# Three RMS norms taken in two columns, eight low-half subtractions given to VectorE, the gathered rows at a multiple of 512 bytes, two constant matrices left out

## The reference

```python
def first_block(x, mem, ...):
    x = x + conv_mixers(rms_norm(x, norm_mix_g[l]), w_in[l], ...)          # gated convolutions, w_mix_out
    x = x + memory_cross_attention(rms_norm(x, norm_xa_g[l]), mem_n, w_q[l], w_kv[l], w_xo[l])
    x = x + peer_ffn(rms_norm(x, norm_peer_g[l]), w_peer_q[l], peer_subkeys[l], peer_u[l], peer_v[l])
    return rms_norm(x, final_norm_g)

def peer_ffn(h, w_pq, subkeys, u, v):
    ...   # 8 heads; each token picks 16 of 16384 experts per head by two top-16 lists of 128 sub-keys
    act = gelu(einsum('chkd,cd->chk', u[experts], h)) * gates
    return einsum('chk,chkd->cd', act, v[experts])

def second_block(x, positions, ...):
    h = rmsnorm(x, pre_norm_mix)
    ...   # windowed attention and latent attention, two gates
    x = x + rmsnorm(merged @ w_out, post_norm_mix)
    y = square(relu(rmsnorm(x, pre_norm_mlp) @ w_up)) @ w_down
    return x + rmsnorm(y, post_norm_mlp)

def rms_norm(x, g):
    return x * rsqrt(mean(x * x, axis=-1) + 1e-6) * g
```

## Time and profile before

| | |
|---|---|
| three runs | 1491.06, 1491.51, 1495.69 us (median 1491.51) |
| the profiled execution | 1493.7 us, span 1491.9 us |
| mean granted TensorE clock | 0.961 |
| busy: PE, DVE, ACT, POOL | 88%, 66%, 35%, 38% of the span |
| gathered bytes | 268.45 MB |

### The profile page before, as it was taken

How to read it: one execution, slowest core, us unless ns; L and a number is a source line. 1 busy time by engine, 2 the same in 40 slices (tenths; PEclk the granted TensorE clock), 3 DMA queues, 4 the chain that set the end, 5 groups by cost and what they waited for, 6 DMA issues and landing times.

```text
span 1491.9 us, 25940 instructions
## 1 busy us (share of the span) xinstructions
PE 1312.2 (88%) x10024; PEld 1253.7 (84%) x10024; DVE 979.4 (66%) x2091; ACT 519.7 (35%) x990; POOL 561.5 (38%) x348
## 2 busy tenths in 40 slices
PE   6999999999888797796968886878899999889996
PEld 5999999988888797796968786878785889889996
DVE  4679986766688585859585768755424447683574
ACT  4633456445442121211112221211226455434341
POOL 1588843221455455354535364545002000022220
PEclk9999999999999989898999899999999999999999
DMA  6555544452389999999999999999830135245450
GB/s 238 213 192 175 188 168 168 158 196 87 112 327 420 421 422 422 422 422 422 422 420 420 421 420 422 422 422 422 359 142 0 57 114 174 100 156 201 162 195 32
DMA packets 58088, 397.39 MB, mean 266 GB/s; under 512 B 6289, under 2 KB 9873, under 8 KB 10385
## 3 DMA queue, kind: packets, MB, share of 16 engines
q0 software_dynamic: 36864, 268.45, 43.3%
q1 hardware_dynamic: 21136, 127.76, 24.2%
HBM read 395.14 MB, written 1.05 MB: 266 GB/s over the span
## 4 chain that ended last, share of the span: by engine, by line
PE 52%; DMA 21%; DVE 13%; issue 8%; ACT 3%; POOL 2%; DVEq 0%; POOLq 0%; ACTq 0%; SPq 0%
DMA rows_late<-peer_uv_dram,stage 21%; PE bank L703 11%; PE bank L705 11%; PE bank L704 11%; PE bank L677 6%; PE bank L914 6%; DVE rows_late L1870 4%; ACT w_hi L1110 2%; PE bank L689 1%; POOL rows_late L620 1%; PE bank L808 1%; DVE hid L2054 1%; POOL w_lo L516 1%; DVE rstd L1442 1%; PE bank L832 1%
## 5 line engine op out<-in xcount | busy, mean ns | idle before, releaser
L516 POOL TENSOR_TENSOR w_lo<-raw,w_hi 128x2048 fp32r<-128x2048 f32 x49 | 228.7, 4669 | 489.8 <-ACT w_hi L1110 489.8
L914 PE MATMUL bank<-h_norm,rows_late 128*128 128x128 f32 x2816 | 328.8, 279 | 30.3 <-ACT h_norm L1274 30.3
L914 PEld LDWEIGHTS bank<-h_norm,rows_late 128*128 128x128 f32 x2816 | 324.9, 196 | 33.4 <-ACT h_norm L1274 33.4
L1870 DVE SCALAR_TENSOR_TENSOR rows_late<-rows_late,squares 128x1024 f32<-128x1024 f32 x176 | 213.8, 1229 | 134.2 <-DMA rows_late<-peer_uv_dram,stage 125.1
L914 PE MATMUL bank<-h_norm,rows_early 128*128 128x128 f32 x1280 | 176.4, 305 | 94.7 <-ACT h_norm L1274 94.7
L914 PEld LDWEIGHTS bank<-h_norm,rows_early 128*128 128x128 f32 x1280 | 170.3, 219 | 101.2 <-ACT h_norm L1274 101.1
L620 POOL DMA_INDIRECT rows_late<-peer_uv_dram,stage x165 | 196.8, 1193 | 131.7 <-PE bank L914 77.7
L1110 ACT ACTIVATE w_hi<-raw 128x2048 fp32r<-128x2048 f32 x102 | 194.3, 1906 | 59.7 <-PE bank L705 49.7
L703 PE MATMUL bank<-x_hi_b,w_hi 128*128 128x256 f32 x640 | 186.9, 292 | 13.8 <-DVE x_lo_b L1474 4.9
L703 PE MATMUL bank<-x_hi_a,w_hi 128*128 128x256 f32 x672 | 191.6, 285 | 4.7 <-DVE x_lo_a L1472 2.3
L704 PE MATMUL bank<-x_lo_a,w_hi 128*128 128x256 f32 x672 | 190.8, 284 | 0.0
(11 more groups left out here) (303 smaller groups left out, 2016.9 us busy)
## 6 DMA issues: line engine op xcount, KB each, us to landing
raw<-w_in_dram SPq DMA_DIRECT2D x28, 1024.0 KB, 5.0
raw<-w_up_dram SPq DMA_DIRECT2D x16, 1024.0 KB, 4.9
raw<-w_down_dram SPq DMA_DIRECT2D x16, 1024.0 KB, 4.9
rows_late<-w_in_dram SPq DMA_DIRECT2D x10, 1024.0 KB, 13.6
raw<-w_kv_dram SPq DMA_DIRECT2D x8, 1024.0 KB, 4.9
raw<-w_peer_q_dram SPq DMA_DIRECT2D x8, 1024.0 KB, 5.0
raw<-sc_w_out_dram SPq DMA_DIRECT2D x4, 1024.0 KB, 4.9
raw<-cf_w_pw_dram SPq DMA_DIRECT2D x4, 1024.0 KB, 4.9
```

What stands on the lines that cost most here:

```text
L516: api.tensor_tensor(ring(w_lo, i), ring(raw, i), ring(w_hi, i).bitcast(F32), ALU.subtract).then_inc(w_lo_ready[LO_BY[i][0]], 1)
L914: mm = nc.tensor.matmul(ct(Y_ACC[c][t // 4], t % 4, P), expert_rows(k)[:, D + t * P:D + (t + 1) * P], ct(diag, k % DIAGS, P), start=False, ...
L1870: w_.scalar_tensor_tensor(out=row, in0=row, scalar=1.0, in1=h_tok[:, c * D:(c + 1) * D], op0=ALU.mult, op1=ALU.mult, accum_out=pre[:, side ...
```

## The change

It has four parts. (1) `BY_DVE` begins at load 32 ("k", 0) and no longer at load 62: eight subtractions that GpSimd made (loads 32, 35, 38, 44, 47, 50, 53 and 56: the first and last of k, the third of sc, the first and last of mix, the third of q, the second of xo, the first of pq) are VectorE's; loads 40, 41 and 58 to 61 stay with GpSimd by `DVE_BUSY`. (2) For the norms in `BY_TOKEN` the squares are the stationary operand and one column of mean_d the moving one: the mean stands in two columns, one per chunk of tokens. ACT and VectorE work on two elements per partition, and TensorE spreads the two columns over the rows again with two products by the identity, into PSUM, which VectorE reads in its place of rstd. (3) mean_q and mean_kv go; the small norms use mean_d and a scale in the root. (4) With them gone and row_pad in, rows_late begins at byte 61,440, a multiple of 512; rows_early and all else behind it move by the same 704 bytes.

```diff
-BY_DVE = range(LOAD_OF["pq", 12], LOAD_OF["up", 6])
+BY_DVE = range(LOAD_OF["k", 0], LOAD_OF["up", 6])
...
+BY_TOKEN = ("peer", "post_mix", "post_mlp")
...
-        mean_q = sb("mean_q", P)
-        mean_kv = sb("mean_kv", P)
...
+        root_col = sb("root_col", NC)
+        rstd_col = sb("rstd_col", NC)
...
+        sb("row_pad", 64)
         (rows_late,) = shared(("rows_late", ROWS_LATE * 2 * D, F32))
...
+        RSTD_HALVES = [psum[7][:, SEQ + c * P:SEQ + (c + 1) * P] for c in range(NC)]
...
             g.memset(mean_d[:], 1.0 / D).then_inc(filled, 1)
-            g.memset(mean_q[:], 1.0 / 256).then_inc(filled, 1)
-            g.memset(mean_kv[:], 1.0 / 128).then_inc(filled, 1)
...
-                    mm = nc.tensor.matmul(STAT[:, 0:SEQ], mean_d[:], ct(squares, k), start=(k == 0), stop=(k == tiles[-1]))
+                    if name in BY_TOKEN:
+                        for c in range(NC):
+                            mm = nc.tensor.matmul(STAT[:, c:c + 1], ct(squares, k)[:, c * P:(c + 1) * P], mean_d[:, 0:1],
+                                                  start=(k == c == 0), stop=(k == tiles[-1] and c == NC - 1))
+                    else:
+                        mm = nc.tensor.matmul(STAT[:, 0:SEQ], mean_d[:], ct(squares, k), start=(k == 0), stop=(k == tiles[-1]))
                 mm.then_inc(stat_ready, 1)
+
+            def spread(name):
+
+                pe.wait_ge(inverted, BY_TOKEN.index(name) + 1)
+                for c in range(NC):
+                    nc.tensor.matmul(RSTD_HALVES[c], rstd_col[:, c:c + 1].to_broadcast([P, P]), ident,
+                                     start=True, stop=True).then_inc(rstd_spread, 1)
...
             stat_sum("peer")
+            spread("peer")
...
-            lora_stat("kv_square", 1, mean_kv, 0)
+            lora_stat("kv_square", 1, 0)
...
-                s.activation(root_buf[:], STAT[:, 0:SEQ], ACT.Sqrt, bias=eps[:, 0:1]).then_inc(rooted, 1)
+                out, n = (root_col, NC) if name in BY_TOKEN else (root_buf, SEQ)
+                s.activation(out[:], STAT[:, 0:n], ACT.Sqrt, bias=eps[:, 0:1]).then_inc(rooted, 1)
...
-                s.activation(root_buf[:], acc(name, 0), ACT.Sqrt, bias=eps[:, 0:1]).then_inc(acc_freed["act"], 1)
+                s.activation(root_buf[:], acc(name, 0), ACT.Sqrt, bias=eps[:, 0:1], scale=float(DT // kt)).then_inc(acc_freed["act"], 1)
...
                 dve.wait_ge(rooted, ROOTS.index(name) + 1)
-                link(w_.reciprocal(rstd[:] if to is None else to, root_buf[:]))
+                if name in BY_TOKEN:
+                    w_.reciprocal(rstd_col[:], root_col[:]).then_inc(inverted, 1)
+                    dve.wait_ge(rstd_spread, NC * (BY_TOKEN.index(name) + 1))
+                    return RSTD_PS
+                to = rstd[:] if to is None else to
+                link(w_.reciprocal(to, root_buf[:]))
+                return to
```

More of the change, by code:

```diff
@@ L480, in two_blocks @@
         inverse_ready = sem("inverse_ready")
+        inverted = sem("inverted")
+        rstd_spread = sem("rstd_spread")
         counts = {}
@@ L834, in sum_values @@
                                  start=False, stop=True).then_inc(acc_ready, 1)
-            pe.wait_ge(filled, 6)
+            pe.wait_ge(filled, 4)
             stat_sum("mix")
@@ L948, in _, with lora_stat @@
             rot = k_of("rot")[NOPE:QHB, 0:QHB]
-            def lora_stat(name, kt, ones, first):
+            def lora_stat(name, kt, first):
                 out = open_tile(name, 0)
@@ L954, in lora_stat @@
                     pe.wait_ge(lora_squared, first + k + 1)
-                    mm = nc.tensor.matmul(out[:, 0:SEQ], ones[:], ct(lora_squares, first + k),
+                    mm = nc.tensor.matmul(out[:, 0:SEQ], mean_d[:], ct(lora_squares, first + k),
                                           start=(k == 0), stop=(k == kt - 1))
@@ L1025, in _ @@
                 mm.then_inc(acc_ready, 1)
-            lora_stat("q_square", 2, mean_q, 1)
+            lora_stat("q_square", 2, 1)
             linear_whole("qa", range(2), "w_in_2", 8, 256)
@@ L1051, in _ @@
             stat_sum("post_mix")
+            spread("post_mix")
             for half in range(2):
@@ L1062, in _ @@
             stat_sum("post_mlp")
+            spread("post_mlp")
             assert tile[0] == len(TILES)
@@ L1185, in _ @@
             square("mix", lambda k: act.wait_ge(x_landed[k // 4], 16), x_res)
-            act.wait_ge(filled, 8)
+            act.wait_ge(filled, 6)
             root("mix")
@@ L1323, in square_lora, with root_of_lora @@
                 s.activation(ct(lora_squares, first + n), ct(latent, n), ACT.Square).then_inc(lora_squared, 1)
-            def root_of_lora(name):
+            def root_of_lora(name, kt):
                 wait_tile(act, name, 0)
-                s.activation(root_buf[:], acc(name, 0), ACT.Sqrt, bias=eps[:, 0:1]).then_inc(acc_freed["act"], 1)
+                s.activation(root_buf[:], acc(name, 0), ACT.Sqrt, bias=eps[:, 0:1], scale=float(DT // kt)).then_inc(acc_freed["act"], 1)
             drain("ckv", 0, c_kv[:])
@@ L1336, in _ @@
                 square_lora("cq", i, 1, c_q)
-            root_of_lora("kv_square")
+            root_of_lora("kv_square", 1)
             wait_tile(act, "ka", 0)
@@ L1347, in _ @@
             act.wait_ge(lora_normed, 1)
-            root_of_lora("q_square")
+            root_of_lora("q_square", 2)
             for i in range(2):
@@ L1482, in norm_split @@
             def norm_split(name, src, gain, dst, x):
-                rstd_of(name)
+                by = rstd_of(name)
                 k = NORMS[NORM_AT[name]][1]
@@ L1488, in norm_split @@
                         done(w_.scalar_tensor_tensor(out=ct(dst, i), in0=ct(src, i), scalar=v(gain, i),
-                                                     in1=rstd[:], op0=ALU.mult, op1=ALU.mult), normed)
+                                                     in1=by, op0=ALU.mult, op1=ALU.mult), normed)
                     if i:
@@ L1515, in _ @@
             split_all("h1", h_norm)
-            dve.wait_ge(filled, 6)
+            dve.wait_ge(filled, 4)
             for i in range(8):
```

## The result

The changed kernel takes 1477.13 us (median of four runs, 1476.33 to 1480.8), the kernel before 1493.18 beside it. The ratio is 0.9897, 95% interval 0.9872 to 0.9922: by the ratio 15.4 us, against a forecast of 8.1. The profiled execution has a span of 1475.1 us.

A forecast was written before the change was run, and what follows sets the result against it. The prediction took the gather stage to be bound by its transfers at 421 GB/s, so gains had to come from starting it earlier. Terms -1.3 - 1.3 + 0.7 - 1.7 - 3.3 - 1.2 gave -8.1, 1483.4 us; range 1476 to 1490.

The forecast's parts named there:

- The place of the rows: Gather stage: moving rows_late to an aligned start was taken as 0, with bounds 0 and 2.3%, -14.6 us.
- (b): Rival on the gather stage: alignment pays, 1.9% of 637 us, 12 us more, 1471.5 us; chance 0.12.
- The step of load 38: Sc stage: shorter L1615 operations, less VectorE's own subtraction in line, start it 1.3 us earlier.
- the clock behind it: Behind the sc wait: with idle time at 1.0 us the clock doesn't fall, -1.3 us over 15 products.
- merge: Load 44: a shorter gate_sc against the subtraction in line, less a wait for ACT's half, -0.5 us.
- mix: Load 47: VectorE waits in line for ACT's half with other operations behind it, +1.3 us.
- q: Load 50: first c_buf at 317.4 us, one TensorE wait replacing another; loads 44 to 50 together +0.7 us.
- Xo and the norms: Loads 53 and 56 in xo, -1.7 us; three norms in columns, -1.1 us each, -3.3 in all.
- The clock behind peer: Start of pq: with the idle 4.08 us shortened, the clock should stay at 1.00 from 379 to 382, -1.2 us.
- (a): Rival: VectorE's in-line waits for ACT's halves eat the gain, about +5 against the forecast, 1488.4 us; chance 0.12.
- (c): Rival: the rows' new place costs transfers, 421 falling to 411 GB/s in the gathers, 1499 us; chance 0.06.
- (d): Rival: GpSimd's hold on VectorE isn't what stretches the rows; norms alone give -3.3, 1488 us; chance 0.04.

The follow-up runs named there:

- subs_back: The changed kernel with the eight subtractions given back to GpSimd; 1482.62 us in one time.
- norms_back: The changed kernel with the three norms over 256 columns as before, `spread` left out; 1481.56 us in one time.
- align_only: The changed kernel with subtractions and norms put back as before, keeping the rows' place and the left-out matrices; 1481.82 us, ratio 0.9926 to the kernel before.
- off192: The changed kernel with row_pad of 112 words, so rows_late begins 192 bytes past a multiple of 256; 1489.02 us, ratio 0.9976 to the kernel before.

## Why the prediction was right and where not

The sign held, and so did "faster by more than 0.3%" and the range (1476 to 1490); the likeliest case did not. That the time, 1477.13, lies in the range is in part luck: two errors stood against each other. The place of the rows gave 10 to 12 us where the sum had 0, and the engine parts gave some 4 us where it had 8.1. Rival (b) in full on top of the whole forecast would have been 1471.5, out of the range.

**Sc, merge, mix, q.** Right in mechanism, and close in size. The step of load 38 is -1.3 (forecast) and -1.31; the clock behind it -1.3 and -1.35 in this pair of traces; merge -0.5 and -0.5; mix +1.3 and +1.14; q -0.1 and -0.26. The start of sc itself scatters by a us, so the first of these agrees better than it can be known; the wait shrank by 1.41 us. c_buf 0 came at 314.57 in a kernel that runs 2.0 us early, so it was 0.8 us earlier than the 317.4 that I worked out, and the bank was free in time.

**Xo and the norms.** For xo and the norm peer -1.7 and -1.1 were forecast, together -2.8; measured -2.92, of which subs_back gives 1.8 to the subtractions and norms_back 1.1 to the norm. From root to first scaled tile 2.3 us became 1.26 at post_mix, and 2.36 became 1.75 at post_mlp, where TensorE was at its lower clock in this one execution; the same place took 1.33 us in all nine other kernels with the new norm. So about 1.0 each, as in the sum, and the one-column statistics add 0.1 each in the tail, which I had at 0.

**The clock behind peer** was the first step that failed: "1.92 us left the clock alone, 2.31 did not, so it should stay at 1.00 between 379 and 382". The longest idle time did shrink to 1.70 us, and the clock fell all the same; the term brought 0.16 of 1.2 us in this trace. The length of one idle time doesn't decide it: 1.91 us ahead of the statistic, 2.30 at sc and 2.60 in up were followed by either level in different executions. With the new norm and no fillers the clock was down behind pq's start in all seven kernels, and in five of them for longer than before: 14.5 to 14.7 us from pq to the scores, against 13.5 to 13.9 in the four kernels with the old norm. There the norm lost 0.6 to 1.2 us of its gain again. I had made a rule out of two rows of one execution. With products in the idle time it stayed up, in three kernels of three.

**The place of the rows** was the second: "I take 0". The 6 ns between gather and plain load that I took to be there for no such reason were mostly the price: 4.9 of them went with the new place. The misreading was to take the load from 28 to 29 us, 309 ns, as proof that a start costs nothing: it takes 309.0 ns at either place, while the gathers, and plain loads in line near the end of the gather stage, show the loss. Why that load doesn't is open. The measured 10 to 12 us lie at (b)'s size: 12 forecast, 11 by align_only, 10.2 by the table's gathers.

**The sum of the parts.** The engine parts alone came to 3.6 us (off192, 0.9962 to 0.9989 of before) where I had 8.1. Without the two clock terms the forecast would have been 5.6, which lies at the edge of that interval; the longer stretch of low clock behind peer takes 0.8 more. The rest is not told apart. One kernel's times differ by 5 to 7 us, and the granted clock goes with them: of the nine runs of off192, 1485.05 us had a mean clock of 0.964 and 1492.01 one of 0.951; of the twelve of the kernel before beside them, 1490.92 had 0.962 and 1496.44 had 0.955. So a term of about one us can be read in a trace, between two places of one row, and not from the time of one run.

Rivals (a), (c) and (d) did not come: TensorE's idle time at the fifth tile of q was 0.39 us, the gathers got faster, and both moved parts show their own effect.

## What to carry to other kernels

Price a transfer by transfers of the same kind in a stretch that is as long and as full as the one you ask about: 5 ns in 315 are 10 us over a gather stage at 1.01 DMA share, and one us of a single load didn't show them. Place the target of large gathers at a multiple of 256 bytes. Don't draw a rule for the clock from one execution: look at the same place in several. Where GpSimd subtracts beside VectorE, look for small VectorE operations that stand with several us; moving the work is worth it where VectorE has slack and not where tiles that TensorE waits for stand behind it.

## What the runs showed of the hardware

- Rows of 8,192 bytes gathered to a start 64, 128 or 192 bytes past a multiple of 256 came at 421 GB/s, to a multiple of 256 or 512 at 427, in full flow. Plain loads in line took 39.0 us of the DMA engines' time for a MB before and 38.3 after; a single load took 309.0 ns a packet at both places.
- The same idle time of TensorE (1.91 us ahead of the statistic of peer, 2.30 at sc, 2.60 in up) was followed by a granted clock of 1.00 in some executions and about 0.5 in others, of the same instructions. With products in the idle time around peer and post_mix it was 1.00 behind both in three kernels of three.
- While GpSimd's subtraction of 4.6 to 5.6 us ran, a VectorE operation with two inputs in SBUF, of 0.4 to 0.5 us, stood until it ended (4.26, 4.44, 3.52 us). Operations that read one of their inputs from PSUM took 0.42 and 0.48 us inside it (x_res at 362.08, gate_cf at 273.21 of the kernel before). In the changed kernel, with GpSimd quiet, all of them took 0.4 to 0.5 us.
